# Key blocks turned in pairs in both long attentions of a two-layer fp32 transformer kernel

## The reference, cut to what matters

```
# "mla": 8 heads, query/key width 96, value width 64, causal
sc = einsum('bqhd,bkhd->bhqk', qb, k) * scale
sc = where(key_pos <= query_pos, sc, -inf)
p  = softmax(sc);  o = einsum('bhqk,bkhd->bqhd', p, v)
# "dsa": 8 heads on 2 key/value heads, width 64; the keys of each query are
# the 256 with the highest index score, given to the kernel's stage as a mask
sc = einsum('bqkgd,bqjkd->bqkgj', qg, kg) * scale
p  = softmax(where(valid, sc, -inf));  o = einsum(..., p, vg)
```

## Time and profile before

| | |
|---|---|
| median of the runs shown | 3289.93 us |
| profiled execution, its own time | 3295.96 us |
| its span | 3294.2 us |
| TensorE busy | 3113.1 us (95%), 17304 matmuls |
| VectorE busy | 2027.1 us (62%) |
| ScalarE busy | 1834.8 us (56%) |
| GpSimd busy | 841.3 us (26%) |
| mla attention, first to last matmul | about 440.2 to 915.9 us |
| dsa attention, first to last matmul | about 1570.1 to 2003.2 us |
| mean granted TensorE clock | 0.972 of 2.4 GHz |

### The profile page before, as it was taken

How to read it: one execution, slowest core, us unless ns; L and a number is a source line. 1 busy time by engine, 2 the same in 40 slices (tenths; PEclk the granted TensorE clock), 3 DMA queues, 4 the chain that set the end, 5 groups by cost and what they waited for, 6 DMA issues and landing times. The chain is left out here.

```text
span 3294.2 us, 51770 instructions
## 1 busy us (share of the span) xinstructions
PE 3113.1 (95%) x17304; PEld 2653.0 (81%) x17304; DVE 2027.1 (62%) x4677; ACT 1834.8 (56%) x3869; POOL 841.3 (26%) x1362
## 2 busy tenths in 40 slices
PE   6999969999999999998799998999999999879998
PEld 5888858888878777776678777999788888779997
DVE  5767667888855666654689897433456666641112
ACT  5656557777766666664688774211256666632211
POOL 5353511122112122232322111111034444311110
PEclk9999979999999999999899999999999999989999
DMA  4666673536342232233531104444432222243342
GB/s 167 209 192 209 186 177 71 119 73 136 108 167 78 72 91 76 72 88 98 137 84 33 32 22 140 145 148 154 149 130 73 58 76 68 70 154 124 109 128 77
DMA packets 307577, 370.49 MB, mean 112 GB/s; under 512 B 24833, under 2 KB 252081, under 8 KB 303345
## 3 DMA queue, kind: packets, MB, share of 16 engines
q1 hardware_dynamic: 292272, 319.72, 33.6%
q0 software_dynamic: 13152, 46.32, 4.4%
q10 hardware_dynamic: 1888, 1.15, 0.1%
HBM read 216.32 MB, written 150.80 MB: 111 GB/s over the span
## 5 line engine op out<-in xcount | busy, mean ns | idle before, releaser
L93 PE MATMUL i_p_g<-i_hT_lo,i_wh 128*128 128x512 f32 x768 | 309.9, 403 | 6.3 <-PEq L70 6.3
L94 PE MATMUL i_p_g<-i_hT_hi,i_wl 128*128 128x512 f32 x768 | 307.8, 401 | 0.0
L95 PE MATMUL i_p_g<-i_hT_hi,i_wh 128*128 128x512 f32 x768 | 307.6, 400 | 0.0
L1786 DVE SCALAR_TENSOR_TENSOR i_score<-i_relu,i_w,i_score 128x1024 f32<-128x1024 f32 (+7 forms) x154 | 155.3, 1025 | 170.9 <-ACT i_relu L1666 169.1
L1676 ACT ACTIVATE i_above<-i_score,i_less 128x2048 bf16<-128x2048 f32 (+13 forms) x140 | 183.1, 1308 | 105.9 <-POOL i_less L1740 69.6
L1126 DVE TENSOR_TENSOR mla_tl<-mla_p_x,mla_th 128x512 fp32r<-128x512 f32 (+1 forms) x320 | 194.2, 609 | 67.9 <-ACT mla_th L1171 62.0
L1171 ACT ACTIVATE mla_th<-mla_p_x 128x512 fp32r<-128x512 f32 (+1 forms) x320 | 168.1, 528 | 85.4 <-PE mla_p_x L1078 83.1
L1126 DVE TENSOR_TENSOR dsa_tl<-dsa_p_x,dsa_th 128x512 fp32r<-128x512 f32 x272 | 186.7, 689 | 46.7 <-ACT dsa_th L1171 41.5
L1163 ACT ACTIVATE dsa_probs<-dsa_probs,dsa_shift 128x640 f32<-128x640 f32 (+7 forms) x192 | 172.0, 896 | 51.0 <-POOL dsa_shift L1195 46.9
L1163 ACT ACTIVATE mla_probs<-mla_probs,mla_shift 128x640 f32<-128x640 f32 (+4 forms) x192 | 171.9, 895 | 32.3 <-POOL mla_shift L1195 27.6
L1666 ACT ACTIVATE i_relu<-i_p_s 128x1024 f32<-128x1024 f32 (+7 forms) x176 | 141.6, 813 | 79.9 <-PE i_p_s L1634 41.5
(11 more groups left out here) (349 smaller groups left out, 9863.3 us busy)
## 6 DMA issues: line engine op xcount, KB each, us to landing
scratch_gates<-i_ob SPq DMA_DIRECT2D x95, 256.0 KB, 2.4
m_m<-scratch_gates SPq DMA_DIRECT2D x64, 256.0 KB, 3.9
f_hs<-scratch_h2T SPq DMA_DIRECT2D x16, 1024.0 KB, 9.3
scratch_qkT<-b_th SPq DMA_DIRECT2D x64, 192.0 KB, 2.6
i_ws<-in_w_in SPq DMA_DIRECT2D x24, 512.0 KB, 4.6
scratch_qkT<-b_tl SPq DMA_DIRECT2D x60, 192.0 KB, 2.9
b_xt<-in_x SPq DMA_DIRECT2D x16, 512.0 KB, 4.8
scratch_h<-b_xh POOLq DMA_DIRECT2D x16, 512.0 KB, 3.0
```

The costliest lines, as they stand in the source:

```text
L93: pe.matmul(out, l[0], r[1], start=start, stop=False)
L94: pe.matmul(out, l[1], r[0], start=False, stop=False)
L95: return pe.matmul(out, l[0], r[0], start=False, stop=stop)
L1786: nc.vector.scalar_tensor_tensor(out=acc, in0=r, scalar=w[:, t, h:h + 1], in1=acc, op0=ALU.mult, op1=ALU.add).then_inc(summed, 1)
```

## The change

Two edits. In `schedule`, no score piece is placed ahead of a block with an odd number, nor directly behind a V; such pieces wait for the next tick. In `stage_attention`, TensorE no longer multiplies after every block, but only after odd blocks and after the last of a unit, as many as are needed to bring the lag back to 3.

```diff
@@ schedule
     for x, tick in enumerate(ticks):
-        while pieces and pieces[0][0] <= x:
+        joined = x and (ticks[x - 1][0] == "V" or tick[0] == "B" and tick[2] % 2)
+        while not joined and pieces and pieces[0][0] <= x:
             take_scores()
@@ stage_attention, TensorE
                     behind.append((n, place, j, s0))
-                    if len(behind) > layer.lag:
-                        multiply()
+                    if place % 2 or place == len(units[n]["blocks"]) - 1:
+                        while len(behind) > layer.lag:
+                            multiply()
```

## The result

| | before | after |
|---|---|---|
| median | 3290.44 us (4 runs, 3288.07 to 3291.6) | 3343.63 us (4 runs, 3342.73 to 3351.92) |
| ratio, 95% interval | | 1.0171 (1.0154 to 1.0187) |
| span of the profiled execution | 3294.2 us | 3350.1 us |
| mla, first to last matmul | 475.4 us | 498.8 us |
| dsa, first to last matmul | 432.7 us | 470.2 us |

The change costs 53.2 us. 3307 was predicted, with a range that ended at 3330. Both attentions lose, dsa more: +37.5 us against +23.4 in mla; the other stages were 5 us shorter in this one execution.

What follows compares the result with a forecast made beforehand. TensorE was taken to set the pace in both attentions. Pairs 0, mla's unit starts +10, dsa's +8, multiplying in pairs 0, less 1 for bank waits, gave +17 us on 3289.93: 3307 us, range 3291 to 3330.

Steps and rivals of the forecast that it cites:

- What bounds the kernel: Both attentions: TensorE sets the pace, VectorE close behind in dsa at 89% busy.
- Part 1: TensorE's block pairs: eight transposes in a row save nothing, 1.80 us a pair against 1.78; 0 us, bounds +-6.
- Rival 1: TensorE's pairs: each saves 0.09 us at the changeover and the fifth transpose costs nothing more; 3281 us, chance 0.06.
- Part 2, mla's unit starts: First transposes of mla's units: moved score pieces shorten the cover more than the chain; +10 us, bounds 0 and 37.
- Part 2, dsa's unit starts: First transposes of dsa's units: mean cover falls from 5.0 to 4.1 us, chain hardly shortens; +8 us, bounds 0 and 18.
- against it I set 4 us: dsa's unit starts: 4 us taken off, as TensorE's new waits let VectorE catch up and the next chain begin earlier.
- Part 3: Multiplying in pairs: rounding of odd blocks waits 0.55 us longer but is covered, and six banks suffice; 0 us, bounds 0 and 158.
- The prediction's own sign of this: Inside units: TensorE waiting for `tl` or banks by over 5 us more would show the prediction wrong.
- The sum: Whole kernel: 0 + 10 + 8 + 0, less 1 for bank waits in units 9 and 10, +17 us; 3307 us.
- Rival 3: dsa's pairs: bursts starve VectorE, idle 0.25 us more each, 32 us on top of 17; 3339 us, chance 0.12.
- Rival 2: Unit starts: chains begin earlier by as much as the covers shrink; 3290 +- 6 us, chance 0.14.
- Rival 4: TensorE's long rows of transposes: the clock falls, costing some 85 us in dsa; 3390 us, chance 0.02.

Runs made afterwards that it cites:

- Short `tl`: VectorE's subtraction for the low part cut to 128 columns at most from the 65th block on: changed kernel 3311.7 us, kernel before 3274.5 us.

## Why the prediction was wrong, point by point

- **What bounds the kernel**: right. TensorE sets the pace, and what the change costs is waits of TensorE.
- **Part 1, eight transposes in a row, 0 us**: right, though its count was too high. The changed list has 160 and 128 pairs, but 29 and 13 of them stood in the list before, so 246 are new and not 288. A pair takes 1.80 us, and the kernel with the schedule edit alone, in which matmuls stand between the transposes again, takes no less than the changed one (3347.1 and 3343.6). Rival 1 (3281) is out.
- **Part 2, mla's unit starts, +10 us**: right; 5.1 to 15.5, and unit 29 at 3.65 us. The mechanism is the one described, but the sum owes a little to luck: units 26 to 30 gained 0.1, 0.7, 0.4, 0.8 and 0.6 us where 0.3, 0.3, 0.3, 0.8 and 0.75 had been worked out, and unit 25, put at 0, lost its 0.5.
- **Part 2, dsa's unit starts, +8 us**: wrong, +18.3, my upper bound. In unit 19 the wait went up by 1.5 us instead of 0.8. The step that failed is "against it I set 4 us: each new wait of TensorE lets VectorE catch up". The maximum came later, not earlier (2.02 to 2.75 us in unit 19, 2.15 to 2.89 on average), because the last piece stands behind two `tl` instead of one. Where VectorE is relieved, the loss is 10.3, near the 12 that the covers alone gave.
- **Part 3, 0 us**: its first half, the rounding that waits for the multiplication of b-4, was right; the edit alone takes 1.0001 of the time. Its second half failed, and it is the largest error: "a bank is now asked for again about 3.4 us after it was filled at the tightest, against a VectorE time of 0.7 for each step". A bank isn't free when VectorE has worked on it for 0.7 us, but when ScalarE's queue has come to the rounding as well: 4.2 us after it was filled in unit 16. The trace of the kernel before already had 31 blocks of dsa over 3.4 us. Inside units this costs 14 us in mla and 20 in dsa; I had put 0 and -1. The prediction's own sign of this, over 5 us more of such waits, came true.
- **The sum**: unit starts +10.4 + 18.3, inside units +14.0 + 19.8, in all 62.5 us by the two traces, whose other stages differ by some -5. Their spans differ by 55.9 us and the medians by 53.2: the profiled execution after was the longest of its four.
- **Rival 3** (3339) had the time nearly right and part of the reason: VectorE does matter, for some 16 us. But it isn't starved by TensorE's rows of transposes (0.25 us for each pair); it waits for ScalarE's rounding (75.2 us in dsa, 35.6 before), and ScalarE for the shift (73.7 and 46.9). **Rival 2** is out. **Rival 4**: the clock did fall, for moments, not at the rows of transposes but behind waits. Windows of the kernel after, two in mla and three in dsa:

```profile
588.50:591.00 2.50, 2.50 (x9) 2.05 (x8) 2.50 (x7) 1.93 (x5) 0.30 (x2) 0.53 1.06 249
833.50:836.50 3.00, 3.00 (x10) 2.42 (x10) 3.00 (x9) 2.22 (x5) 0.49 (x3) 0.50 1.00 243
1690.00:1694.00 4.00, 4.00 (x16) 3.52 (x15) 2.32 (x6) 2.65 (x6) 0.29 (x1) 0.58 0.03 7
1970.00:1974.00 4.00, 4.00 (x16) 3.32 (x15) 3.07 (x8) 0.60 (x1) 0.29 (x1) 0.59 0.00 0
2042.00:2046.00 4.00, 4.00 (x17) 3.33 (x16) 2.33 (x5) 1.48 (x3) 3.53 (x2) 0.63 0.00 0
```

The granted clock there is at or near the lower level, 1.2 GHz. Ahead of the first two TensorE had waited 1.10 and 0.53 us, and 1.09 and 0.53, within two microseconds; ahead of the three in dsa once, for 1.33, 1.96 and 3.49 us. 2.5 x 0.47 + 3.0 x 0.50 + 4.0 x (0.42 + 0.41 + 0.37) = 7.5 us in all. The same stages before have no such stretch (1.00 in the earlier trace rows), so some 7 of the 62.5 us of excess are the lower clock and not waits, most of them inside units. Over the whole of both windows the clock is 0.99, with rows of eight transposes throughout and of twelve at unit starts. The Trainium skill ("TensorE: Matmul & The Clock Gate", section "Part 4: PE-mode transpose") says that transposes don't engage the full clock; in rows of this length between matmuls, the trace doesn't agree (0.99).

What stays open: how the 34 us inside units divide. In mla 9.4 of the 14.0 need GpSimd's output work; in dsa 11.4 of the 19.8 go when the exponentials stand later in both kernels. Short `tl` takes off 6.0 and 8.7. The parts overlap, and no run takes all of them away together.

## What to carry to other kernels

- When steps are regrouped in a fixed order over several in-order engines, follow each buffer of a ring through *all* engines until it is free, with what stands ahead in each queue. The time that the last engine works on it is only the least that it can take. The trace of the kernel before shows how long buffers are really held; look there first.
- A cost beside which the engine in question isn't seen to wait can still set the end two engines further on; a cut of that engine's work tells it, and only with the same cut in the kernel before is it known to belong to the change.
- Cover lost at a known chain could be worked out here to half a microsecond for a unit; the same chain's own start must be walked too, for it can move in the wrong direction.

## Not expected of the hardware

- The granted clock fell to half, for some 3 us each time, behind waits of 1.1 and 0.53 us close together (588.5 and 833.5 us), and behind single waits of 1.33, 1.96 and 3.49 us, in stretches that were otherwise full of matmuls.
- GpSimd's two output instructions (0.61 and 1.28 us for 64x512): cutting them to an eighth is worth 25 us of 3290, with GpSimd 26% busy. Moving them behind a shift is worth 11 us in the order of before and 4 in the changed one.
